# Down weights of a 32-expert layer: asked for on ScalarE's queue instead of SyncE's

## The reference, cut to what matters

```python
t = rmsnorm(x, g2).reshape(-1, 1024)
gates = ...                       # coarse group, then the best two of its eight experts: (tokens, 32), two non-zero a row
for e in range(32):
    h = silu(t @ w_gate[e]) * (t @ w_up[e])          # 1024 -> 512
    y = y + (h * gates[:, e, None]) @ w_down[e]      # 512 -> 1024
x = x + y
```

## Time and profile before

| | us |
|---|---|
| median of 3 runs | 702.96 |
| lowest and highest | 701.39, 705.41 |
| the profiled execution, its own time | 701.98 |
| its span | 700.2 |
| PE busy | 667.3 (95%) |
| DVE, ACT, POOL busy | 298.4, 111.0, 45.5 |
| start of the first turn's `gate_up` | 224.21 |
| end of the last down product | 683.14 |

### The profile page before, as it was taken

The page is one execution under the profiler, slowest core; times in us unless marked ns, Lnnn a source line. Parts: engine busy times, 40 slices in busy tenths (PEclk is TensorE's granted clock), DMA queues, the critical chain, the costliest instruction groups (busy, mean ns, idle before and its releaser), DMA issues.

```text
span 700.2 us, 8831 instructions
## 1 busy us (share of the span) xinstructions
PE 667.3 (95%) x3770; PEld 372.4 (53%) x3770; DVE 298.4 (43%) x532; ACT 111.0 (16%) x203; POOL 45.5 (7%) x48
## 2 busy tenths in 40 slices
PE   7999999999988999999999999999998999889995
PEld 4999999887864343443434434444343333333432
DVE  5646238612438234335424433354233433323345
ACT  6421253301420001000100010001000001000005
POOL 2000000000002010001000100010000100000001
PEclk9999999999979999999999999999999999999998
DMA  9940600088258999999999999999999999999963
GB/s 289 347 131 3 241 1 1 1 342 328 83 173 330 411 422 419 418 421 418 419 419 420 420 418 419 420 420 418 418 420 418 421 419 419 419 421 420 420 249 135
DMA packets 45515, 229.82 MB, mean 328 GB/s; under 512 B 7876, under 2 KB 15061, under 8 KB 21155
## 3 DMA queue, kind: packets, MB, share of 16 engines
q1 hardware_dynamic: 42915, 224.52, 79.6%
q0 software_dynamic: 2560, 4.73, 1.9%
HBM read 228.03 MB, written 4.85 MB: 333 GB/s over the span
## 4 chain that ended last, share of the span: by engine, by line
PE 60%; SPq 20%; DMA 13%; DVE 5%; ACT 2%; issue 1%; DVEq 0%
PE ps L1511 17%; SPq L499 14%; PE ps L1349 13%; DMA w<-in_moe_w_up 12%; PE ps L1533 9%; PE ps L1420 8%; SPq L505 6%; PE ps L1548 5%; PE ps L1446 1%; PE ps L1522 1%; DVE hexT L1193 1%; PE ps L1313 1%; PE ps L1315 1%; PE ps L1314 1%; DMA gain<-in_norm_g 1%
## 5 line engine op out<-in xcount | busy, mean ns | idle before, releaser
L1511 PE MATMUL ps<-w,xT 128*64 128x512 f32 x1024 | 227.6, 593 | 12.9 <-DMA w<-in_moe_w_up 12.2
L1511 PEld LDWEIGHTS ps<-w,xT 128*64 128x64 f32 x1024 | 72.4, 137 | 162.8 <-issue 139.4
L843 DVE TENSOR_TENSOR x_sb<-ps,x_sb 128x512 f32<-128x512 f32 (+1 forms) x166 | 106.4, 681 | 42.3 <-PE ps L1420 32.7
L1533 PE MATMUL ps<-wd,hexT 128*64 128x512 f32 x512 | 116.9, 598 | 2.5
L843 DVE TENSOR_TENSOR hexp<-silu_g,ps 128x256 f32<-128x256 f32 x32 | 13.5, 420 | 197.9 <-ACT silu_g L797 197.9
L1533 PEld LDWEIGHTS ps<-wd,hexT 128*64 128x64 f32 x512 | 33.9, 136 | 65.0 <-issue 55.2
L1548 PE MATMUL ps<-y_hi,home 64*128 64x512 f32 (+1 forms) x320 | 66.6, 410 | 1.6 <-DVE y_lo L849 1.6
L1548 PE MATMUL ps<-y_lo,home 64*128 64x512 f32 (+1 forms) x320 | 63.2, 389 | 0.0
L603 POOL DMA_INDIRECT xg<-hn_rows,idx x32 | 35.9, 1121 | 371.9 <-PE ps L1501 353.8
L801 ACT ACTIVATE y_hi<-ps,gate_of 128x512 fp32r<-128x512 f32 x32 | 22.0, 687 | 212.1 <-PE ps L1533 212.1
L1349 PE MATMUL ps<-hT_hi,wi_hi 128*128 128x288 f32 x224 | 48.7, 299 | 0.0
(11 more groups left out here) (210 smaller groups left out, 582.8 us busy)
## 6 DMA issues: line engine op xcount, KB each, us to landing
wd<-in_moe_w_down SPq DMA_DIRECT2D x64, 1024.0 KB, 25.8
w<-in_moe_w_gate SPq DMA_DIRECT2D x63, 1024.0 KB, 25.7
w<-in_moe_w_up SPq DMA_DIRECT2D x63, 1024.0 KB, 26.7
wo<-in_w_out SPq DMA_DIRECT2D x2, 2048.0 KB, 10.9
x_sb<-in_x_prompt SPq DMA_DIRECT2D x4, 512.0 KB, 8.9
hn_rows<-hn2p SPq DMA_DIRECT2D x4, 512.0 KB, 3.0
out<-x_sb SPq DMA_DIRECT2D x4, 512.0 KB, 2.6
wi_v<-in_w_in SPq DMA_DIRECT2D x4, 384.0 KB, 8.0
```

Of the source, the lines that this page charges most:

```text
L843: return nc.vector.tensor_tensor(out, a, b, op)
L1511: last = mm(ps[64 * h:64 * h + 64, 1, :], lhs, w1[s][:, :, k, h * (F // 2):(h + 1) * (F // 2)], start=(k == 0), stop=(k == KD - 1))
L1533: last = mm(ps[64 * h:64 * h + 64, 3, :], lhs, wd[s][:, c, h * 512:(h + 1) * 512], start=(c == 0), stop=(c == F // P - 1))
```

## The change

The two down loads of experts 3 to 31 are taken out of SyncE's loop and issued by ScalarE, on ScalarE's own DMA queue, in program order right behind the `y_hi` of expert n - 3. They are the same transfers into the same buffers with the same semaphores. ScalarE has already waited for `dn_ps` there, for `y_hi`. SyncE's loop keeps the gate and up loads and their two waits. The down loads of experts 0 to 2 stay with SyncE, and so do those of the second path.

```diff
@@ sync: for n in range(NSLOT, NE)
                     load_last_quarters(n, s)
                 else:
                     load_gate_up(n, s, halves=(1,))
-                sp.wait_ge(main["dn_ps"], done)
-                load_down(n, s, second=wd_last if n == NE - 1 else None)
@@ scalar
+            down_v = w_down[0].rearrange("e (h p r) d -> p e h (r d)", p=P, r=2)
+
+            def load_down(e, s):
+
+                for half in range(2):
+                    act.dma_start(wd[s][:, 2 * half:2 * half + 2, :].rearrange("p (o c) d -> p o (c d)", o=1),
+                                  down_v[:, bass.ds(e, 1), half, :]
+                                  ).then_inc(wd_last if e == NE - 1 and half else wd_in[s], 16)
+
             def block_first(n):
                 silu(main, n)
                 if n == 0:
                     act.wait_ge(routed, 1)
                 high(main, n, n + 1, n % 3, gate_of[:, n:n + 1])
+                if n + NSLOT < NE:
+                    load_down(n + NSLOT, n % NSLOT)
```

## The result

The changed kernel takes 711.48 us (median of 4 runs, 711.27 to 715.27) against 703.02 us (4 runs) for the kernel before: ratio 1.0136, 95% interval 1.0095 to 1.0177 (worked out from all runs; the medians alone give 1.0120). That is slower by 8.5 us in the medians; the forecast was 712.9 us, in a range of 707 to 718. The profiled execution took 711.27 us, its span is 709.4 us.

The account below looks back on a forecast made before the run. The prediction took the full DMA engines, 419 GB/s, as the bound. Bytes 0, SP 0, ACT 0 and load order 9.9 sum to 9.9 us: 701.98 becomes 711.9, median 712.9 us (1.0 above), range 707 to 718.

Parts of the forecast that it names:

- The stream is full and its end stays: Weight loads in the expert stage: engines already full at 419 GB/s, last load still lands at 678.4 us.
- SP's issues gain nothing: Two DMA issues a turn leave SP, held only because its queue is full; nothing starts later for it: gain 0.
- ACT's issues cost nothing: Two issues a turn behind `y_hi` take 0.7 us of ACT's 6.18 us before the next silu: cost 0.
- The rival of a held ACT: ACT waits out SP's held issues, losing up to 9.2 us a turn; time up to 733; chance 0.06 for over 718.
- Equal turns between the queues: Each queue gets half the rate while both have work; downs land about 10 us after issue, displacing gate/up: +9.9 us.
- The rival of service in the order of asking: Both queues served in order of asking, down 31 still lands last: no change, within 0.5%; chance 0.09.
- Gate and up keep 25 us or so to landing: Sign of being right: gate and up loads on SP's queue still take 25 us or so from issue to landing.
- PE's release moves by 9.6 us in turn 30: PE's wait for gate/up 30 ends at 668.4 us, 10.0 us before the stream's end; before, PE went on at 658.80.
- the three counts of the forecast: Units behind gate/up 30, 29 and 28 put the last down product's end at 692.7, 693.0 and 692.6 us.
- PE waits 22 us for up, from about 380 us on: PE's waits for up loads over the stage grow from 12.2 to about 22 us, starting about 380 us instead of 520.
- the store: PE's early loads ahead of need, about 20 us at turn 3, eaten at roughly 1 us a turn; half is left.
- Total: Whole kernel: +9.9 us from load order, profiled execution 711.9 us, median 1.0 us above it, 712.9 us.

Follow-up runs that it names:

- e6: Changed kernel with roles swapped: gate and up loads of experts 3 to 31 issued by ACT, downs by SyncE; 714.06 us, ratio 1.0166 to the kernel before.
- e5: Kernel before with only the down pair of expert 31 issued by ACT, all others by SyncE; 708.08 us, ratio 1.0072 to the kernel before.
- e4: Kernel before with down loads of experts 3 to 28 issued by ACT, those of 29 to 31 by SyncE; 710.27 us, ratio 1.0105.
- e9: Changed kernel with down loads of experts 13 to 31 issued two turns later, behind silu; 707.95 us, ratio 1.0078 to the kernel before.
- e3: Kernel before with only the down loads of experts 29, 30 and 31 issued by ACT, the rest by SyncE; 713.82 us, ratio 1.0160.
- e1: Changed kernel with each pair of down loads issued by ACT one turn later; 711.66 us, ratio 1.0135 to the kernel before.
- e2: Changed kernel with each pair of down loads issued by ACT two turns later, behind silu; 709.85 us, ratio 1.0100 to the kernel before.
- e7: Kernel before, one queue, second half of gate and up loaded in 512 KiB quarters for every expert from 3 on; 706.27 us, ratio 1.0040.

## Why the prediction was right, point by point

- *The stream is full and its end stays.* Right within 0.8 us: 419 to 420 GB/s at a share of 1.01, the last load in at 677.9 us. The forecast took 678.4 for the kernel before, with the shortest time to landing of the earlier trace rows; the last load's own was 22.7 us, which gives 678.7.
- *SP's issues gain nothing.* Right in the sum. SyncE spent 293 us at its 176 issues of the stage before, and 184 us at 118 after the change, and the time did not fall. But SyncE is not "rarely held" after the change, as the forecast had it: up to about 380 us its issues are short in both kernels, 0.3 to 0.4 us each, and from 396 us on single ones take up to 4.6 us in both; after the change 52 of the 118 take 1 us or more.
- *ACT's issues cost nothing.* 0.82 us a pair, in the 6.18 us of ACT's wait. No turn of the changed kernel has a late silu in the rows I read. The rival of a held ACT did not come about here; e6 shows that ACT is held with gate and up on its queue, though that did not set the end there.
- *Equal turns between the queues.* Right: 1.93 MB against 1.84 in the 9 us in which both have work. The rival of service in the order of asking fell. By this the Trainium skill's rule of turns between queues ("DMA: Bandwidth & Descriptors", Queues, rings and completion order) agrees with the trace for ScalarE's and SyncE's queues too; how long one turn is, no row here shows. What the forecast left out is the 3.5 us until the first byte. The two loads of the last pair land 9.0 and 14.0 us after their issues, where about 10 was forecast for both.
- *Gate and up keep 25 us or so to landing.* Wrong: 34.8 and 38.9 us at 600 us. They stand in a queue that gets half the rate whenever a pair of downs passes.
- *PE's release moves by 9.6 us in turn 30.* Forecast 668.4, measured 668.05; by then the pair of down 31 is in, with or without the 3.5 us. For turn 29 the forecast was 654.9, and PE went on at 653.16. Here the 3.5 us are the miss: the forecast had 0.6 unit of down 31 moved, and it was 0.06 MB. With 9.9 units behind it instead of 9.4, and the end at 677.9, the count gives 653.2. It decides nothing, because turn 30 alone sets the end; that the three counts of the forecast agreed on 693 was partly luck. e5, e4 and e9 bear out the count from other sides, within 0.2, 0.2 and 1.2 us.
- *PE waits 22 us for up, from about 380 us on.* Measured 16.6 us, 5.4 us less, and the first wait ends at 422 us. The sum is right and its form was not: the missing part is in slower matmuls (next section but one). Why the store lasted 40 us longer was not looked into.
- *Total.* Stage +9.7 us (forecast 9.9), profiled execution 711.27 (forecast 711.9), median 711.48 (forecast 712.9, of which 1.0 was the distance of the profiled execution to the median, and that was 0.2 this time).

What stays open: how much of e3's 1.5 us over the changed kernel the late down loads make, and why the stream of e6 ends 1.4 us later.

## What to carry to other kernels

When the DMA engines are full, a second queue moves no more bytes; it changes who goes first. Loads with a long time until they are needed then overtake those that the compute engine waits for next. So before moving a load to another queue, count the bytes that stand behind the critical load at the moment when it is needed: that count, at the stream's rate, gave the releases to within 2 us where the stream had no gap, and to 0.2 us in the two places where the bytes that had really moved were put in (turn 29 of the changed kernel, turn 30 of e9). Loads just asked for had moved nothing for 3.5 us here, so they count whole. And if a second queue is wanted for another reason, let it ask late where there is a backlog, and early where there is none.

## What the runs showed of the hardware that I had not expected

**The matmuls behind a long wait of PE can run at half the clock.** In the changed kernel some waits are longer than any before (up to 3.0 us against 1.9), and the matmuls behind some of them are slow. PE's timeline, two turns in a row:

```profile
592.14 3.65 PE L1520 MATMUL ps<-w,xT 128*64 128x512 f32 x16 [1.12 <-DMA w<-in_moe_w_up]
...
608.34 5.35 PE L1520 MATMUL ps<-w,xT 128*64 128x512 f32 x16 [2.46 <-DMA w<-in_moe_w_up]
```

and the windows in and behind the second one (PEclk, DMA share, GB/s last):

```profile
610.00:612.00 2.00, 2.00 (x8) 0.53 (x6) 0.00 (x0) 0.00 (x0) 0.00 (x0) 0.50 1.00 418
612.00:614.00 2.00, 2.00 (x12) 0.63 (x10) 0.00 (x0) 0.26 (x1) 0.00 (x0) 0.98 1.01 422
```

The granted clock is 0.50 of full speed, the lower level of 1.2 GHz, and 16 matmuls take 5.35 us instead of 3.65: 1.7 us more. It happened three times in the changed kernel, after waits of 2.99, 2.48 and 2.46 us, and adds up to 5.1 us, which is the part missing from the waits (16.6 + 5.1 = 21.7). It did not follow every long wait: after one of 2.41 us the 16 matmuls took 3.65 us, and in e9 so did those after one of 2.97. In the kernel before none was slow. While the stream is the bound, later waits are shorter by what the slow matmuls took, so the end hardly moves: the two turns behind 608.34 run without a wait, and in the third, at 653.16, PE waits for its load again. Some versions with long waits spread more: e1 took 708.96 to 714.77 us at mean granted clocks of 0.984 to 0.975, while the 7 runs of the kernel before beside it took 701.24 to 705.24 us at 0.984 to 0.991. But e2, with a wait of 3.5 us in its profile, stays within 1.3 us. That the clock makes the spread, and with it the other order of e1 and e2 in the medians, is likely and not shown.

**Loads of 512 KiB with rows of 4 KiB moved fewer bytes a second than loads of 1 MiB with rows of 8 KiB**, with the engines as busy. e7 moves 415 to 416 GB/s against 419, 1% less, with a third of its bytes in such loads; if these alone are slower, they are so by 2.5%, an estimate from the same numbers. Whether the rows or the number of loads do it is not told apart here.
